# Moving one-tile work of a mixer into the chunk stage, and a new order of the products of two neighbouring tiles

## What is computed

```python
def ssd_scan(x, dt, Bm, Cm, A, h0, with_output):
    a_cs = jnp.cumsum(dtc * A, axis=2); a_end = a_cs[:, :, -1]
    w_end = jnp.exp(a_end[:, :, None] - a_cs) * dtc
    chunk_states = einsum('bcjh,bcjhn,bcjhp->bchpn', w_end, Bc, xc)
    # step over the chunks: h = exp(a_end) * h + chunk_state; h_in is the state ahead of each
    scores = einsum('bcihn,bcjhn->bcijh', Cc, Bc) * decay_ij * dtc[:, :, None, :, :]
    y = einsum('bcijh,bcjhp->bcihp', scores, xc) + einsum('bcihn,bchpn->bcihp', Cc, h_in) * exp(a_cs)[..., None]

def gla_scan(q, k, v, g, S0, with_output):
    b = jnp.cumsum(g, axis=2); b_end = b[:, :, -1]
    chunk_states = einsum('bcjhk,bcjhv->bchkv', kc * exp(b_end[:, :, None] - b), vc)
    q_dec, k_inv = qc * exp(b), kc * exp(-b)
    attn = where(causal, einsum('bcihk,bcjhk->bchij', q_dec, k_inv), 0.0)
    o = einsum('bchij,bcjhv->bcihv', attn, vc) + einsum('bcihk,bchkv->bcihv', q_dec, S_in)

def merge_heads(m, y_ssd, o_gla, p):
    y = rmsnorm((y_ssd + d_skip * m['x']) * silu(m['z']), ssd_norm_g)
    o = rmsnorm(o_gla, gla_norm_g) * silu(m['g_out'])
    return concatenate([y, o]) @ p['w_out']
```

## Time and profile before

| | us |
|---|---|
| median of 3 runs (lowest, highest) | 2832.84 (2830.89, 2845.7) |
| the profiled execution | 2829.67 |
| its span in the profile | 2827.9 |
| PE busy in the span | 2456.4 (87%) |
| DVE, ACT, POOL busy | 1546.5, 1064.9, 529.4 |
| mean granted clock of TensorE | 0.892 of full |

### The profile page before, as it was taken

One profiled execution on the slowest core, in us unless ns is written; L12 is line 12 of the kernel. 1 busy time (PEld: TensorE's weight loads), 2 busy tenths in 40 slices (PEclk: granted clock), 3 DMA queues, 4 the chain that ended last, 5 costly groups with the idle time before them and its releaser, 6 DMA issues. The chain is left out here.

```text
span 2827.9 us, 36830 instructions
## 1 busy us (share of the span) xinstructions
PE 2456.4 (87%) x12303; PEld 1857.3 (66%) x12303; DVE 1546.5 (55%) x1960; ACT 1064.9 (38%) x1315; POOL 529.4 (19%) x535
## 2 busy tenths in 40 slices
PE   2999999999999796689998883299999999999990
PEld 1677567656665564577777772278888888888880
DVE  1322122222212344555555555199999999999993
ACT  0112112121212121322222220177777777777772
POOL 1000000000000001112212212523333333333332
PEclk7899999989999676689999996599999999999995
DMA  8122212111210567444444436144789876989976
GB/s 315 56 69 80 92 41 84 73 61 65 98 43 12 215 216 263 178 161 161 168 161 161 162 109 217 41 151 135 227 286 311 271 251 208 364 264 355 316 258 260
DMA packets 174733, 492.19 MB, mean 174 GB/s; under 512 B 11504, under 2 KB 26251, under 8 KB 167467
## 3 DMA queue, kind: packets, MB, share of 16 engines
q1 hardware_dynamic: 150971, 407.67, 39.3%
q0 software_dynamic: 23664, 83.18, 11.9%
HBM read 382.16 MB, written 108.65 MB: 174 GB/s over the span
## 5 line engine op out<-in xcount | busy, mean ns | idle before, releaser
L578 PE MATMUL pz<-w_in_sb,hT 128*128 128x512 f32 x800 | 367.9, 621 | 0.0
L548 PE MATMUL pf<-hT,w_in_sb 128*128 128x256 f32 x1440 | 331.1, 395 | 1.1 <-DVE hT L637 1.1
L548 PEld LDWEIGHTS pf<-hT,w_in_sb 128*128 128x128 f32 x1440 | 286.7, 200 | 42.8 <-DVE hT L637 1.5
L1912 ACT ACTIVATE w_hi_e<-w_gates 128x2048 fp32r (+1 forms) x103 | 197.6, 1919 | 236.4 <-issue 103.1
L578 PEld LDWEIGHTS pz<-w_in_sb,hT 128*128 128x128 f32 x800 | 158.1, 200 | 191.9 <-issue 191.5
L2038 DVE TENSOR_TENSOR w_lo_e<-w_gates,w_hi_e 128x2048 fp32r<-128x2048 f32 x103 | 236.7, 2299 | 33.3 <-ACT w_hi_e L1912 33.3
L2038 DVE TENSOR_TENSOR w_lo_e<-w_ups,w_hi_e 128x2048 fp32r<-128x2048 f32 x102 | 233.4, 2288 | 35.6 <-ACT w_hi_e L1912 35.6
L2038 DVE TENSOR_TENSOR w_lo_e<-w_downs,w_hi_e 128x2048 fp32r<-128x2048 f32 x100 | 228.2, 2282 | 0.0
L1912 ACT ACTIVATE w_hi_e<-w_ups 128x2048 fp32r (+1 forms) x102 | 195.2, 1914 | 23.8 <-PE pd_e L1985 22.6
L1912 ACT ACTIVATE w_hi_e<-w_downs 128x2048 fp32r x100 | 191.1, 1911 | 3.0 <-issue 0.3
L1985 PE MATMUL pg_e<-w_hi_e,x_hi_e 128*128 128x512 f32 x408 | 167.3, 410 | 7.2 <-DVE w_lo_e L2038 7.2
(11 more groups left out here) (348 smaller groups left out, 4285.9 us busy)
## 6 DMA issues: line engine op xcount, KB each, us to landing
w_gates<-in_w_gate_dram SPq DMA_DIRECT2D x32, 2048.0 KB, 11.5
w_ups<-in_w_up_dram SPq DMA_DIRECT2D x32, 2048.0 KB, 16.6
w_downs<-in_w_down_dram SPq DMA_DIRECT2D x32, 2048.0 KB, 10.3
tok_rec<-tm SPq DMA_DIRECT2D x8, 2960.0 KB, 9.6
rec_m<-tok_rec SPq DMA_DIRECT2D x16, 1288.0 KB, 7.2
rec_s<-tok_rec SPq DMA_DIRECT2D x18, 968.0 KB, 6.7
w_mod_half<-in_w_mod_dram SPq DMA_DIRECT2D x16, 1024.0 KB, 7.9
abc_m<-a_rows SPq DMA_DIRECT2D x16, 1024.0 KB, 9.9
```

Source lines behind the costliest of these rows:

```text
L548: mm = pe.matmul(pf[n % 2][:, f, :], w[:, k, c0:c0 + P], h[:, k, :], start=(k == 0), stop=(k == KT - 1))
L578: mm = pe.matmul(pz[n % 2][:, :], h[:, k, s * P:(s + 1) * P], w[:, k, o:o + 512], start=(k == 0), stop=(k == KT - 1))
L1912: act.activation(w_hi[:, s % 3:s % 3 + 1, :], raw(part, half, place), ACT.Copy).then_inc(hi_done, 1)
```

## The change

Three things change.

One-tile work moves from the mixer to the chunk stage: the scores of B and C with their mask (now `masked_scores`, two operations of 256), and the cumulative sums of the gates, their exponentials and the products with q and k (`grow`, `decayed_qk`). They are stored to a new DRAM tensor `qk_rec` (768 KB a tile) that the mixer loads. The decays at the chunks' ends are now columns of `grow`, where there were products with `halves`. `w_out` is also prepared there, one of its 8 blocks a tile from tile 3 on. `small` and the new `sums_t` have one buffer each. The mixer no longer loads the gate part of `tok_rec` nor five of the six pieces of `feat_rec`.

PE's order in a slot of the mixer becomes `attn(now)`, `ssd(now)`, `turned_m(before)`, `gla(now)`, `turned_x(done)`, `project(before)` whole, `router(done)`; `turned_m` turns a tile whose o was made in the slot ahead. DVE prepares the segments and scores of tile n+1 in slot n. In `attn`, `gla` and `products` the order of the 64-row products changes.

The mixer's loads: `load(n+1)` is issued in slot n, right behind `load_abc(n+1)`, its first piece waiting for `next_done` in the first two; z and the output gate are loaded apart (`zg`). `h_rows` is filled a tile a slot.

```diff
@@ chunks, SP
             for i in range(TILES):
...
-                sp.wait_ge(fwd_done, 2 * i + 2)
-                sp.wait_ge(ends_done, 2 * i + 2)
+                sp.wait_ge(fwd_done, 4 * i + 4)
...
                 if i + NR < TILES:
-                    sp.wait_ge(back_ps, i + 1)
+                    sp.wait_ge(fwd_ps, i + 1)
                     sp.wait_ge(xw_done, i + 1)
-                    sp.dma_start(rec[i % NR][:, :], tok_rec[at(i + NR)][:, 0:T_Z]).then_inc(loaded[i % NR], 16)
+                    if i >= CT:
+                        sp.wait_ge(qk_done, 2 * (i - CT) + 2)
+                    load(i + NR)
+                if i >= CT:
+                    sp.wait_ge(qk_done, 2 * (i - CT) + 2)
+                    sp.wait_ge(scm_done, 2 * (i - CT) + 2)
+                    sp.dma_start(qk_rec[at(i)], qk[i % 2][:, :, :, :].rearrange("p a b c -> p (a b c)")).then_inc(qk_stored[i % 2], 16)
+                if NW <= i < KT:
+                    sp.wait_ge(w_lo_done, i - NW + 1)
+                    load_w(i)
@@ chunks, ACT, exponentials(i)
+                act.activation(grow[i % 3][:, :, :], g, ACT.Exp).then_inc(grow_done, 1)
+                if i >= CT:
+                    if i >= CT + 2:
+                        act.wait_ge(qk_stored[b], stores(i, b, 2))
+                    act.activation(qk[b][:, 1, :, :], g, ACT.Exp, scale=-1.0).then_inc(grow_done, 1)
@@ chunks, PE
+                if i >= 1:
+                    pe.wait_ge(ends_done, 3 * i)
+                    pe.wait_ge(grow_done, i + max(0, i - CT))
...
             def products(i):
...
+                if i - 1 >= CT:
+                    pe.wait_ge(scm_done, 2 * (i - 1 - CT) + 2)
@@ chunks, DVE, loop
                 if j >= 1:
                     weighted(j - 1)
+                    decayed_qk(j - 1)
                 if j >= 2:
                     states(j - 2)
+                    masked_scores(j - 2)
+                if W0 < j <= W0 + KT:
+                    low_w(j - W0 - 1)
+                if W0 <= j < W0 + KT:
+                    gated_w(j - W0)
@@ mixer, SP
                 if now is not None and now + 1 < LT:
                     sp.wait_ge(lag_done, 4 * now + 4)
                     load_abc(now + 1)
+                    if before is not None:
+                        sp.wait_ge(o_ps, before + 1)
+                        sp.wait_ge(next_done, before + CT + 1)
+                    load(now + 1)
+                    if before is not None:
+                        sp.wait_ge(o_done, before + 1)
+                    load_zg(now + 1)
                     sp.wait_ge(y_ps, now + 1)
                     load_cs(now + 1)
                 if before is not None:
                     sp.wait_ge(x_added, 2 * before + 2)
                     sp.dma_start(x_mid_t[before], x1[before % 2][:, :]).then_inc(x1_stored[before % 2], 16)
-                if now is not None and now + 2 < LT:
-                    sp.wait_ge(o_ps, now + 1)
-                    sp.wait_ge(o_done, now + 1)
-                    sp.wait_ge(next_done, now + CT + 1)
-                    load(now + 2)
                 if before is not None and before + 2 < LT:
                     sp.wait_ge(xs_done, before + 1)
@@ mixer, PE, loop
                 if now is not None:
-                    scores(now)
+                    attn(now)
+                    ssd(now)
                 if before is not None:
-                    turned_m(before)
+                    turned_m(before, 0)
+                    turned_m(before, 1)
+                if now is not None:
+                    gla(now)
                 if done is not None:
                     turned_x(done)
                 if before is not None:
-                    project(before, range(0, 4))
+                    project(before, range(KT))
                 if done is not None:
                     router(done)
-                if now is not None:
-                    ssd(now)
-                    attn(now)
-                if before is not None:
-                    project(before, range(4, KT))
-                if now is not None:
-                    gla(now)
@@ mixer, DVE, loop
                 if now is not None:
-                    masked_scores(now)
-                    segment(now, 0)
+                    masked_attn(now)
+                    state_mid(now + CT, now)
+                    state_next(now + CT, now)
                 if before is not None:
-                    split_m(before)
+                    split_m(before, 0)
+                    split_m(before, 1)
                 if now is not None:
-                    segment(now, 1)
-                    decayed_scores(now)
-                    decayed_qk(now)
-                    decayed_c(now)
-                    state_mid(now + CT, now)
+                    gated_y(now)
+                if more:
+                    segment(now + 1, 0)
+                    segment(now + 1, 1)
+                if now is not None:
+                    gated_o(now)
+                if more:
+                    decayed_scores(now + 1)
+                    decayed_c(now + 1)
+                if before is not None:
+                    residual(before)
+                    scaled_x(before)
                 if done is not None:
                     logits(done)
...
```

More of the change, by code:

```diff
@@ L773, in _, with load, load_w @@
             sp.dma_start(nega[:, SH:], A["a_log_b"].to_broadcast([P, SH])).then_inc(a_loaded, 16)
+            def load(i):
+                sp.dma_start(rec[i % NR][:, :], tok_rec[at(i)][:, 0:T_Z]).then_inc(loaded[i % NR], 16)
+                sp.dma_start(feat[i % NR][:, :, :].rearrange("p a b -> p (a b)"), feat_rec[at(i)]).then_inc(loaded[i % NR], 16)
+            def load_w(k):
+                sp.dma_start(w_raw[k % NW][:, :], A["w_out"][0, k * P:(k + 1) * P, :]).then_inc(w_loaded[k % NW], 16)
             for i in range(NR):
-                sp.dma_start(rec[i][:, :], tok_rec[at(i)][:, 0:T_Z]).then_inc(loaded[i], 16)
+                load(i)
+            for k in range(NW):
+                load_w(k)
             for i in range(TILES):
@@ L857, in products @@
             def products(i):
-                r, k, x = rec[i % NR], kend[i % 2], xw[i % 2]
+                r, k, x, f = rec[i % NR], kend[i % 2], xw[i % 2], feat[i % NR]
                 pe.wait_ge(kend_done, i + 1)
                 pe.wait_ge(xw_done, i + 1)
-                for d, ssd, first, second, done in ((1, b02[:, 0:256], b02[:, 256:512], b1[:, 0:256], back_ps),
-                                                    (0, f01[:, 0:256], f01[:, 256:512], f2[:, 0:256], fwd_ps)):
+                if i - 1 >= CT:
+                    pe.wait_ge(scm_done, 2 * (i - 1 - CT) + 2)
@@ L863, in products @@
+                for d, ssd, first, second, sc, done in ((1, b02[:, 0:256], b02[:, 256:512], b1[:, 0:256], b1[:, 256:256 + P], back_ps),
+                                                        (0, f01[:, 0:256], f01[:, 256:512], f2[:, 0:256], f2[:, 256:256 + P], fwd_ps)):
                     if i:
-                        pe.wait_ge(*((next_done, i) if d else (fwd_done, 2 * i)))
+                        pe.wait_ge(*((next_done, i) if d else (fwd_done, 4 * i)))
+                    if i >= CT:
+                        g = 1 - d
+                        pe.matmul(sc, f[64 * g:64 * g + 64, 0, :], f[64 * g:64 * g + 64, 1, :], start=True, stop=True)
@@ L867, in products @@
                                   start=True, stop=True)
[L868 to L869 removed]
+                    for h in range(GH):
+                        for c, to in ((0, second), (1, first)) if d else ((0, first), (1, second)):
                             mm = pe.matmul(to[64 * (h % 2):64 * (h % 2) + 64, P * (h // 2):P * (h // 2 + 1)],
@@ L958, in ps @@
             return ctx.enter_context(nc.psum_tensor(f"{name}_m", [P, 2, 512], F32))
-        rec = [sb(f"rec{b}", [P, M_LEN]) for b in range(2)]
-        feat = [sb(f"feat{b}", [P, F_TILES, P]) for b in range(2)]
+        rec = [sb(f"rec{b}", [P, M_GF]) for b in range(2)]
+        zg = [sb(f"zg{b}", [P, 2, SW]) for b in range(2)]
+        qks = [sb(f"qks{b}", [P, 3, 4, P]) for b in range(2)]
+        cT = [sb(f"cT{b}", [P, P]) for b in range(2)]
         bst = [sb(f"bst{b}", [P, 3, 256]) for b in range(2)]
```

396 lines of the change are left out of this document (190 added, 206 removed).

## The result

The changed kernel takes 2868.94 us (median of 4, 2865.1 to 2871.45) against 2836.2 (median of 4, 2830.89 to 2845.7) before: a ratio of 1.0114, 95% interval 1.0078 to 1.015. It is 33 us (1.1%) slower, where I had forecast a gain, 2780. The profiled execution is a run of 2869.2 us with a span of 2867.4, 39.5 more than before.

A forecast was written before the change was run, and what follows sets the result against it. PE was taken to bound the mixer before, the loads' loop after. Chunk stage +56, ramp -46.5, mixer loads -65 and tail +4.5 gave -51 us: forecast 2780, range for 8 in 10 2700 to 2830.

The forecast's parts named there:

- Step 1: Chunk stage, engine work: a tile stays about 8 us, hidden by PE; up to 4.7 us more at 1.2 GHz.
- Step 2: Chunk stage, new `qk` store with two buffers: tiles of 12.5 us (bounds 9.5 and 13), +56 us in all.
- Q: Chunk stage: the time at which the `qk` store that the next exponential waits for has landed.
- Step 3: Mixer, ramp: earlier scores and no wait for weights or fills bring `ssd(2)` to 1174.5 from 1220.87, -46.5 us.
- Step 4: Mixer, PE work: stalls and moved products gone, a tile would take about 27 us were PE the bound.
- Step 5: Mixer, loads one tile ahead: landing plus DVE's chain makes 29.6 us a tile instead of 34.6, -65 us.
- Step 6: Tail after the last `ssd`: all of `project(14)` and a router come behind it, against one stall less, +4.5 us.
- B: Mixer: lost prefetch, loads landing at X + 21, 35.6 us a tile, 2858, slower than before; chance 0.11.
- X: Mixer: the end of `xs` of tile n-2, after which SP issues the next loads.
- C: Chunk stage at 1.2 GHz, tiles of 15 us, and mixer landing at X + 16: 2821, about no change; chance 0.12.
- A: Chunk tiles of 9.5 us (-33) or mixer loads landing by X + 12.4 (-34): either 2747, both 2713; chance 0.35.

The follow-up runs named there:

- the version with all three mends: Changed kernel with three buffers for the growth products, their store ahead of the two loads, and the mixer's record loads two tiles ahead: 2670.6 us, ratio to before 0.9442.

## Why the prediction was wrong, step by step

**Step 1, engine work of the chunk stage: the sum right, the word hidden wrong.** 12.6 us a tile at half clock was worked out from two rows; 12.58 was measured. But I called this hidden and named its loss as a possible cost only, though the granted clock was 0.72 in the stage as it was. In the changed kernel the store's wait covers it; with that wait taken away, it is most of what is left of the stage's loss, 198.6 against 154.6 us.

**Step 2, the new store: the loop is as described, its length isn't (51 us forecast, 84 measured).** ACT, DVE and PE wait in the order I gave, and the masks end 4.3 us after the landing, 4.2 by my sum. The store's issue came at Q + 5.1 (4.4), since SP takes 0.4 to 0.9 us for each of the loads ahead of it, and the landing 9.7 us after issue (8.6 at Q + 13). That is 14.8, above my upper bound of 13; I had then taken 12.5, below the ordered case, with a trace in which such loads land in order. And I counted eleven turns where twelve gaps from 963.62 to 1143.38 are 14.3 to 15.6: tiles 2 to 13 store behind loads, which is twelve. 12 x (15.0 - 8.0) = 84, and from the last tile's first product to the mixer 27.3 us instead of 18.2: +92.6 with rounding.

**Step 3, the ramp: right, in part by luck.** -46.8 against -46.5. The first `ssd` comes 29.9 us after the stage's first product, 30.4 by my sum, but two terms offset each other: the loads were issued 12.6 us in and not 14.4, and the segments with POOL beside them took 6.3 us and not 4.9 (1204.24 to 1210.52).

**Step 4, PE's work: too high.** 27.0 stood against a measured 24.86. I gave the new order of the 64-row products a worth of 0 to 1.5 and took 0; `gla` takes 3.3 us (1448.76 to 1452.03 in the kernel with early loads) in place of 4.8, and `attn` 1.1 in place of 1.6 (1370.20 to 1371.80, timeline of before): 2.0 of the 2.1 us. The Trainium skill, "TensorE: Matmul & The Clock Gate", Part 3: Packing small matmuls, says that a weight load overlaps a running product only where their row groups differ, which is what the new innermost loop makes of neighbours; the 1.5 us agree. It did not matter to the result, since PE was not the bound.

**Step 5, the loads' loop: the right loop, four terms too short.** Landing 17.3 instead of 15. The sum had 4.8 MB ahead of it, addition and fill among them, and put what SP issues behind `bst` (z and gate, and `cs`, 1.0 MB) at nothing. The windows and the bytes of SP's queue (packets, MB, share) from the end of `xs` to the landing, and then those of the 14.8 us of before:

```profile
1471.95:1489.20 17.25, 16.16 (x112) 13.13 (x110) 5.50 (x14) 4.54 (x15) 3.58 (x6) 1.00 0.95 309
q1 hardware_dynamic: 1162, 4.28, 64.7%
```

```profile
1352.09:1366.90 14.81, 13.79 (x72) 12.00 (x73) 10.99 (x19) 4.64 (x8) 0.00 (x0) 0.77 0.85 309
q1 hardware_dynamic: 864, 4.08, 67.4%
```

The rate is the same, 309 GB/s, so it isn't that the engines were slower. Of SP's queue the sum had counted 3.76 MB, and 4.28 were moved (4.30 to 4.48 in four other tiles); before, the loads that I had counted are the whole of the 4.08. So some 0.5 MB of what was issued last moved before the last load that the segments wait for was there: 1.7 us at that rate. No run tests this by holding those loads back. The other 0.6 is that 4.8 MB at 309 GB/s is 15.5 us and not 15. Contention 2.5 instead of 1.3. Segments 3.9 (0.68 to 0.69 each, the six of them without conflict) where I had 3.6. And squares, root and `scaled_x` took 4.0 where I had 3.7. 29.6 + 2.3 + 1.2 + 0.3 + 0.3 = 33.7, the measured turn. Every one of the four is off the same way, and the loop adds them up thirteen times: that is the 51 us.

The Trainium skill's rule on the lock of the shared port ("SBUF — State Buffer", Who interferes with whom), which I had set aside for a row of the ramp, gave 3.1 in all, 1.8 over the 1.3 that I took. The traces of after and of the experiments show 2.5, so two thirds of the way to the rule: POOL's three products take 3.98 us there (2.49 for two and 1.49), and DVE is held for 2.5 of them where all three meet its work, and for 1.7 where they meet it in part (4.18 for 2.49 above). I had called the rule's price unsupported because of one meeting in the ramp (1.15 and 1.52), which was two instructions long; in the steady mixer it is three.

**Step 6, the tail: +8.8 for +4.5.** PE's waits in the tail didn't grow: 2.24 and 3.15 us for the last two `xs` (at 1736.46 and 1755.22), where it had stood 3.69 for the last `o` and 4.86 for the last `xs`. What I had put at nothing is the clock: the last `ssd` comes behind PE's idle and takes 10.6 us with the states' products (to 1714.04), where it had taken 5.5 (1671.44 to 1676.96).

```profile
1703.41 7.09 PE L1363 MATMUL py_m<-xd_m,M_m 128*128 128x64 f32 x32
```

**The rivals.** B, a landing still later than forecast, holds 2.3 of the 4.1 us a tile by which step 5 was short, though it stayed 2.9 us below the X + 20.2 from which it would decide alone. C had the number of the chunk tile, 15 us, by luck: it put the 15 down to PE's clock, and with the store's wait gone a tile at that clock takes 12.58. Its landing was 1.3 us short, and it was 48 us too fast, since it kept the eleven turns and the short chain. A, to which I gave 0.35, needed the store to overtake loads of its own queue, or the mixer's loads to land 5 us sooner than they did. My range ended at 2830 because even C, with both loops longer, reached only 2821: the store's landing, the turns, the conflict and the chain behind the landing had no price above my own sum in any case.

## What to carry to other kernels

In these runs a transfer that an engine waited for cost the queue ahead of it (9.7 us against 4.5), and in the mixer some of what was issued behind it too. Before adding a store with few buffers, write down what the same queue is given between the data's last write and the store's issue, and put the store first. When work is moved ahead, see which load now becomes the first need, and give it its old distance or, if that can't be, a semaphore of its own. Here the third buffer, the store ahead and the old distance turned a kernel 1.1% slower than before into one 5.6% faster; the semaphore took 5.3 us off a tile alone and nothing on top of them. The terms of a loop of waits are taken at their far ends, since the loop repeats every error; here all four of step 5 had the same sign.

## What the runs showed of the hardware that I had not expected

- **TensorE at half clock with no idle.** In the windows shown, PE is busy for 30.00 of 30 us, twice in a row, at a granted clock of 0.50 (1.2 GHz); in the kernel with three buffers a stretch from 990 to 1060 us is busy for 70.00 of 70 at 0.50. The mixer of the version with all three mends has 0.98 with PE as busy (345.00 of 345, 1185 to 1530 us). So a PE without idle rows can stay at 1.2 GHz in this stage. What brings the clock back here is open: the same code got 0.8 in another execution, 18 us shorter in this stage.
- **A conflict that moves along.** 2.4 to 2.5 us a tile of DVE held by POOL, in the segments (4.51 for 2.07) or in the decayed scores (5.03 for 2.49). With PE as the bound it costs nothing: with the loads two tiles ahead the decayed scores take 4.18 and the tile stays 24.86.
- **What is issued last moves before what is awaited has landed.** In five tiles of the changed mixer SP's queue had moved 0.5 to 0.7 MB more by the landing than the 3.76 MB issued up to the load awaited.
- **A wait can be hidden by a wait.** `gla` behind the output product cost 3.9 us a tile where the loads were late and 12.6 where they were early.
